# Two layers of differential attention in three step groups a head instead of four steps, on new mixing units and merge units

## The chip, the cores and the metric

The kernel runs on one core of one Trainium2 chip, as one program. The metric is the time on the device in microseconds (us), the median of several runs. An earlier stage (a transformer block with sparse attention, retention and a gated feed-forward part) comes first and takes the first third of the span; two more layers of another kind follow. The change touches only these two layers.

## The reference, cut to what matters

A layer makes a pooled branch, a convolution branch and an attention branch, gates and merges them, and goes on with an MLP. All of it is in float32. The attention is the part that the change regroups:

```python
def diff_attention(q1, q2, k1, k2, v, lam):       # S=512, 4 heads, d=64, dv=128
    nb = s_ // Q_BLOCK                            # Q_BLOCK = 128: four query blocks
    scale = d_ ** -0.5
    key_chunk = jnp.arange(s_) // CHUNK           # CHUNK = 64

    def one_block(args):
        qb1, qb2, bi = args
        q_chunk = (bi * Q_BLOCK + jnp.arange(Q_BLOCK)) // CHUNK
        mask = key_chunk[None, :] <= q_chunk[:, None]

        def probs(q, k):
            s = jnp.einsum('bhqd,bhkd->bhqk', q, k).astype(jnp.float32) * scale
            return jax.nn.softmax(jnp.where(mask, s, NEG_INF), axis=-1)

        att = probs(qb1, k1) - lam * probs(qb2, k2)
        return jnp.einsum('bhqk,bhkd->bhqd', att.astype(v.dtype), v)
    ...
# in each of the two layers, from proj = rms_norm(h) @ w_in:
    y_a = multiscale_pool(a_in, pool_w, pool_scale)          # windows 2, 4, 8, 16
    y_b = c_b * causal_depthwise_conv(c_c * c_x, conv_w)
    y_c = (rms_norm(diff_attention(...), sub_norm_g) * (1.0 - lam_init))
    merged = g_a * (y_a @ w_pool_out) + g_b * (y_b @ w_conv_out) + g_c * (y_c @ w_attn_out)
    h = h + merged @ w_o
```

Query block i sees the keys of blocks 0 to i, so its step works on 128, 256, 384 or 512 columns.

## The kernel before

**Units.** All big products are cut into units of 1024 weight columns in SBUF. A weight goes through three engines before TensorE uses it: SyncE loads it into `raw`, ScalarE copies it rounded to `w_hi` (L414), GpSimd subtracts to get `w_lo` (L357), and TensorE runs for each of 8 tiles three matmuls of 128x512: L775, L776 and L777. So a unit is 24 matmuls. ScalarE makes `w_hi` three units ahead, at the place in its own program that belongs to the current unit (`ahead`), and only when TensorE is done with the unit that had the buffer. GpSimd has nothing but `w_lo` to do in these layers, four instructions a unit.

**The mixing stage.** In each layer 16 mixing units ("slots" 0 to 15, `L_MIX`) make the inputs of the pooled and the convolution branch. They alternate between two PSUM banks, so slot j may start only when VectorE has taken slot j-2 out of its bank (L1279, in `mix_in`). VectorE runs in the order of its own loop over k: at k it takes out slot k-1 and works on it (`mix`). The slots 0, 2, 4 and 6 hold the pooled groups 3, 2, 1 and 0: a chain of 4, 3, 2 and 1 window additions (L1962), then L1968, L1972 and L1975, which writes `rg`. At tile 3 of slots 2, 4, 6 and 8 TensorE stops for a matmul that reads this `rg` (L1195). The slots 8 to 15 are four pairs "c" and "b" of the convolution.

**The merge stage.** 36 merge units follow (n = 0 to 35), 12 for each of three branches. In each six, four are gate projections and two are products with the branch outputs. Into this stage VectorE also places, in layer 0, the final norm of the earlier stage (`late_norm`): squares at n = 1, 2, 3, 7 and 8 (L2047, L2051), which TensorE sums at n = 9 by a matmul at tile 1 (L810).

**The attention steps.** Four heads of four steps are spread over both stages. A step goes around all engines:

- TensorE `attention_scores` (L1137): two score products, one for each half of the difference, into the two banks of `both`
- VectorE `step_maxima`: mask on the diagonal block (L1465), maximum (L1468), its negative scaled (L1471)
- ScalarE `softmax_step` (L528): an exponential with its sum for each half
- VectorE `step_probs`: reciprocal of the sums (L1925), second half scaled by lambda (L1927), the difference (L1930)
- TensorE `attention_transposes` (L1149), at tile 5 of a slot; ScalarE copies them to `pt` (L537); TensorE `attention_values` (L1161), after the slot. It issues the scores of the next step first.

In the mixing stage VectorE does step k/2 at every even k, around the `mix_in` of that k; the transposes and values stand at every odd slot. In the merge stage VectorE does a step at n = 0, 3, ..., 21 and TensorE closes it at n = 2, 5, ..., 23. After the last step of a head, `attention_out` copies the head's sum out (L2006) and squares it (L2009); TensorE sums the squares (L810) at tile 7 of slot 8 and at tile 6 of n = 1 and 13, and ScalarE's root of it goes on to `head_inverse` and `head_out`.

No scheduler is at work: each engine's order is the order in which its code is written, and an engine that waits holds back all that stands behind it.

## Time and profile before

| | |
|---|---|
| median of 3 runs | 2618.01 us (2617.67 to 2618.27) |
| the profiled execution | 2617.76 us |
| its span, first to last instruction | 2616.0 us |
| TensorE busy with matmuls | 2579.2 us, 99% of the span |
| VectorE busy | 1564.7 us, 60% |
| GpSimd busy | 1515.9 us, 58% |
| ScalarE busy | 840.2 us, 32% |
| mean granted TensorE clock | 0.998 |

The execution's own time is 1.76 us more than its span. "Busy" of TensorE counts overlapping matmuls once. The mixing stage of layer 0 runs from about 989 to 1098 us of the span and that of layer 1 from about 1838 to 1947 us; the merge stages follow each. In the timeline a row gives the start, the duration, the engine, the source line, what is written and read, how many instructions are merged into the row, and in brackets how long the engine sat idle before it and what ended that.

### The profile page before, as it was taken

The numbers are of one execution on the slowest core, as the hardware profiler recorded it, in microseconds if no ns is written. First come the engines' busy times: TensorE is split into PE (matmuls) and PEld (weight loads), VectorE is DVE, ScalarE is ACT, GpSimd is POOL, SyncE is SP. The second block draws the span as 40 slices with busy tenths as digits, with TensorE's granted clock in tenths as the row PEclk, the third lists the DMA queues.
The fourth block names the chain that finished last, engine by engine and source line by source line (L and its number), as shares of the span: only waits on it lengthen the run. The fifth ranks groups of instructions, "written<-read, shape, count | busy, mean of one in ns | idle before, by whom it ended". The sixth has DMA issues, their size and how long they took to land.

```text
span 2616.0 us, 32859 instructions
## 1 busy us (share of the span) xinstructions
PE 2579.2 (99%) x11707; PEld 2066.1 (79%) x11707; DVE 1564.7 (60%) x2092; ACT 840.2 (32%) x1156; POOL 1515.9 (58%) x1820
## 2 busy tenths in 40 slices
PE   7999999999999999999999999999999999999999
PEld 6767777888888877777888888877777788888887
DVE  6767774388474768855584432757883548443274
ACT  5444433233222332355321111134334432111112
POOL 6634436566666754545566655764454556665576
PEclk9999999999999999999999999999999999999999
DMA  5311113222322222122222222232222222222223
GB/s 195 122 49 59 55 65 113 97 81 96 113 96 97 97 103 81 66 96 81 105 97 97 97 96 96 96 113 88 80 69 92 97 92 94 104 97 93 96 96 125
DMA packets 36829, 247.44 MB, mean 95 GB/s; under 512 B 4464, under 2 KB 4848, under 8 KB 7792
## 3 DMA queue, kind: packets, MB, share of 16 engines
q1 hardware_dynamic: 34704, 238.57, 25.5%
q10 hardware_dynamic: 2016, 7.35, 0.8%
q8 instruction: 76, 1.25, 0.2%
q14 instruction: 33, 0.27, 0.0%
HBM read 243.81 MB, written 2.10 MB: 94 GB/s over the span
## 4 chain that ended last, share of the span: by engine, by line
PE 86%; DVE 9%; ACT 2%; POOL 1%; issue 1%; DMA 1%; DVEq 0%; ACTq 0%; SPq 0%
PE bank L775 17%; PE bank L777 17%; PE bank L776 17%; PE both L775 10%; PE both L777 9%; PE both L776 9%; PE bank L810 1%; POOL w_lo L357 1%; PE both L958 1%; DMA raw<-stream 1%; DVE small L1468 1%; PE bank L945 1%; PE both L1137 1%; PE bank L1161 1%; PE bank L977 1%
## 5 line engine op out<-in xcount | busy, mean ns | idle before, releaser
L357 POOL TENSOR_TENSOR w_lo<-raw,w_hi 128x256 fp32r<-128x256 f32 x1784 | 1493.5, 869 | 1003.6 <-ACT w_hi L414 1003.1
L414 ACT ACTIVATE w_hi<-raw 128x1024 fp32r<-128x1024 f32 x446 | 469.0, 1057 | 989.4 <-PE bank L777 495.1
L775 PE MATMUL bank<-a_hi,w_hi 128*128 128x512 f32 x1544 | 631.6, 409 | 4.2 <-POOL w_lo L357 4.2
L777 PE MATMUL bank<-a_hi,w_lo 128*128 128x512 f32 x1544 | 603.3, 391 | 0.0
L776 PE MATMUL bank<-a_lo,w_hi 128*128 128x512 f32 x1544 | 602.4, 390 | 0.0
L775 PEld LDWEIGHTS bank<-a_hi,w_hi 128*128 128x128 f32 x1544 | 290.4, 188 | 77.4 <-issue 16.3
L776 PEld LDWEIGHTS bank<-a_lo,w_hi 128*128 128x128 f32 x1544 | 290.8, 188 | 63.2 <-issue 7.9
L777 PEld LDWEIGHTS bank<-a_hi,w_lo 128*128 128x128 f32 x1544 | 290.2, 188 | 62.7
L775 PE MATMUL bank<-y_hi,w_hi 128*128 128x512 f32 x696 | 272.4, 391 | 0.0
L777 PE MATMUL bank<-y_hi,w_lo 128*128 128x512 f32 x696 | 270.9, 389 | 0.0
L776 PE MATMUL bank<-y_lo,w_hi 128*128 128x512 f32 x696 | 270.8, 389 | 0.0
L775 PE MATMUL both<-a_hi,w_hi 128*128 128x512 f32 x656 | 259.5, 396 | 0.8 <-DVE a_lo L1771 0.5
L777 PE MATMUL both<-a_hi,w_lo 128*128 128x512 f32 x656 | 255.4, 389 | 0.0
L776 PE MATMUL both<-a_lo,w_hi 128*128 128x512 f32 x656 | 255.3, 389 | 0.0
L775 PE MATMUL both<-y_hi,w_hi 128*128 128x512 f32 x504 | 197.3, 391 | 4.6 <-DVE y_lo L1594 2.7
L777 PE MATMUL both<-y_hi,w_lo 128*128 128x512 f32 x504 | 196.8, 391 | 0.0
L776 PE MATMUL both<-y_lo,w_hi 128*128 128x512 f32 x504 | 196.7, 390 | 0.0
L776 PEld LDWEIGHTS bank<-y_lo,w_hi 128*128 128x128 f32 x696 | 130.7, 188 | 27.4 <-issue 0.5
L777 PEld LDWEIGHTS bank<-y_hi,w_lo 128*128 128x128 f32 x696 | 130.6, 188 | 27.3
L775 PEld LDWEIGHTS bank<-y_hi,w_hi 128*128 128x128 f32 x696 | 130.6, 188 | 27.3 <-issue 0.5
L775 PEld LDWEIGHTS both<-a_hi,w_hi 128*128 128x128 f32 x656 | 123.1, 188 | 29.5 <-issue 2.8
L776 PEld LDWEIGHTS both<-a_lo,w_hi 128*128 128x128 f32 x656 | 123.2, 188 | 27.1 <-issue 2.2
(306 smaller groups left out, 2944.6 us busy)
## 6 DMA issues: line engine op xcount, KB each, us to landing
raw<-stream SPq DMA_DIRECT2D x223, 1024.0 KB, 4.8
h<-xT SPq DMA_DIRECT2D x8, 256.0 KB, 6.0
h<-xT ACTq DMA_DIRECT2D x1, 2048.0 KB, 7.9
outT<-h SPq DMA_DIRECT2D x8, 256.0 KB, 2.3
h<-decay ACTq DMA_DIRECT2D x1, 1024.0 KB, 4.7
h<-rope ACTq DMA_DIRECT2D x1, 1024.0 KB, 9.3
prob<-pT ACTq DMA_DIRECT2D x2, 512.0 KB, 4.2
par<-par ACTq DMA_DIRECT2D x2, 408.0 KB, 2.9
```

The lines of the kernel that those rows point to most:

```text
L357: pool.tensor_tensor(w_lo[:, s, part], raw[:, s, part], w_hi[:, s, part], ALU.subtract).then_inc(lo_done, 1)
L414: act.activation(w_hi[:, s, cols], raw[:, s, cols], ACT.Copy).then_inc(hi_done, 1)
L775: pe.matmul(dst, w_hi[:, s, cols], rhs_hi(k), start=start and k == 0, stop=False)
L776: pe.matmul(dst, w_hi[:, s, cols], rhs_lo(k), start=False, stop=False)
L777: ins = pe.matmul(dst, w_lo[:, s, cols], rhs_hi(k), start=False, stop=stop and k == nk - 1)
L810: pe.matmul((b_r1 if dst is None else dst)[:, :], ones if w is None else w, ssum[:, :] if src is None else src, start=True, stop=True)\
L945: ins = pe.matmul(dst[:, a * P:S], rv[:, a, e * P:(e + 1) * P], rp[:, at:at + n], start=a == 0, stop=a == QT - 1, skip_group_check=True)
L958: ins = pe.matmul(dst[:, 0:n], (q_turned if half != g else qt)[at, cols], k_sw[g][at, 0:n], start=True, stop=True)
L977: ins = pe.matmul(b_o[rows, col], v_sw[g][:, a, rows], pt[:, half, a * P:(a + 1) * P], start=a == 0, stop=a == i, skip_group_check=True)
L1137: ins = pe.matmul(dst[:, 0:n], qn[rows, hd, i * P:(i + 1) * P], kn[rows, hd, 0:n], start=True, stop=True)
L1161: ins = pe.matmul(b_o[:, i * P:(i + 1) * P], vn[:, hd, a, :], pt[:, 0, a * P:(a + 1) * P], start=a == 0, stop=a == i, skip_group_check=True)
L1468: V.tensor_reduce(small[:, 8:10], scores[:, :, 0:n], AX.X, ALU.max)\
```

## The change

The four steps of a head become three groups: steps 0 and 1 together, step 2, step 3. In the first group step 0 has columns 0 to 127 and step 1 columns 128 to 383 of the same banks and tiles. TensorE issues the scores, transposes and values of both steps together. VectorE masks both diagonal blocks in one instruction, takes two maxima, scales four numbers at once, takes four reciprocals at once, and has two instructions of each of the others. ScalarE runs four exponentials and one copy of 384 columns.

There are now 12 groups a layer instead of 16 steps. Six lie in the mixing stage: VectorE does them at k = 0, 3, 5, 8, 11 and 13, and TensorE closes them at slots 2, 4, 7, 10, 12 and 15. Six lie in the merge stage: VectorE at n = 0, 3, 7, 12, 15 and 19, TensorE at n = 2, 6, 11, 14, 18 and 23. Nothing else moves.

```diff
+STEP_GROUPS = [((0, 0), (1, P)), ((2, 0),), ((3, 0),)]
+MIX_STEPS, MIX_VALUES = [0, 3, 5, 8, 11, 13], [2, 4, 7, 10, 12, 15]
+MERGE_STEPS, MERGE_VALUES = [0, 3, 7, 12, 15, 19], [2, 6, 11, 14, 18, 23]
...
+                def attention_step(group):
+                    parts = []
+                    for o, (i, at) in enumerate(STEP_GROUPS[group % 3]):
+                        cols = slice(at, at + (i + 1) * P)
+                        parts += [(prob[:, e, cols], (b_s0, b_s1)[e][:, cols], 2 * o + e) for e in range(2)]
+                    softmax_step(parts, 64 ** -0.5)
...
-                    for e, dst in enumerate((b_s0, b_s1)):
-                        rows = slice(64 * e, 64 * (e + 1))
-                        ins = pe.matmul(dst[:, 0:n], qn[rows, hd, i * P:(i + 1) * P],
-                                        kn[rows, hd, 0:n], start=True, stop=True)
+                    for i, at in STEP_GROUPS[group % 3]:
+                        n = (i + 1) * P
+                        for e, dst in enumerate((b_s0, b_s1)):
+                            rows = slice(64 * e, 64 * (e + 1))
+                            ins = pe.matmul(dst[:, at:at + n], qn[rows, hd, i * P:(i + 1) * P],
+                                            kn[rows, hd, 0:n], start=True, stop=True)
...
+                def step_maxima(group):
+
+                    steps_in = STEP_GROUPS[group % 3]
+                    V.wait_ge(scores_ready, score.due())
+                    blocks = scores.rearrange("p e (b c) -> p e b c", c=P)
+                    first = steps_in[0][0]
+                    diag = blocks[:, :, first:3:2, :] if len(steps_in) > 1 else blocks[:, :, first:first + 1, :]
+                    mask = chunk.unsqueeze(1).unsqueeze(1).to_broadcast([P, 2, len(steps_in), P])
+                    V.tensor_tensor(diag, diag, mask, ALU.add).then_inc(vector_step, steps.up())
+                    V.wait_ge(vector_step, steps.now())
+                    for o, (i, at) in enumerate(steps_in):
+                        V.tensor_reduce(small[:, 8 + 2 * o:10 + 2 * o], scores[:, :, at:at + (i + 1) * P],
+                                        AX.X, ALU.max).then_inc(vector_step, steps.up())
...
-                    if k % 2 == 0:
-                        step_maxima(k // 2)
+                    if k in MIX_STEPS:
+                        step_maxima(MIX_STEPS.index(k))
                     if k > 0:
                         mix_in(k - 1)
                     if k < 2:
                         qk_out(6 + k)
-                    if k % 2 == 0:
-                        step_probs(k // 2)
+                    if k in MIX_STEPS:
+                        step_probs(MIX_STEPS.index(k))
```

VectorE at k = 0 of the mixing stage of layer 0, before: from the mask of step 0 (`both<-both,cst`) to the first window addition (`tb<-ta`) of pooled group 3.

```order
L1465 TENSOR_TENSOR both<-both,cst 128x2x128
L1468 TENSOR_REDUCE small<-both 128x2
L1471 TENSOR_SCALAR small<-small 128x2
L1891 RECIPROCAL tb<-tb 128x512
L1894 SCALAR_TENSOR_TENSOR work<-ta,par,tb 128x512
L1925 RECIPROCAL small<-small 128x2
L1927 TENSOR_SCALAR prob<-prob,small 128x128
L1930 SCALAR_TENSOR_TENSOR prob<-prob,small 128x128
L1279 TENSOR_TENSOR ta<-bank,rstd 128x512
L1891 RECIPROCAL tile_c<-tile_c 128x512
L1894 SCALAR_TENSOR_TENSOR work<-td,par,tile_c 128x512
L1962 TENSOR_TENSOR tb<-ta 128x512
```

The same stretch after the change, up to the reciprocal behind `mix_in` of slot 0 (L1292 now):

```order
L1940 TENSOR_TENSOR both<-both,cst 128x4x128
L1943 TENSOR_REDUCE small<-both 128x2 x2
L1947 TENSOR_SCALAR small<-small 128x4
L1904 RECIPROCAL tb<-tb 128x512
L1907 SCALAR_TENSOR_TENSOR work<-ta,par,tb 128x512
L1956 RECIPROCAL small<-small 128x4
L1960 TENSOR_SCALAR prob<-prob,small 128x128
L1960 TENSOR_SCALAR prob<-prob,small 128x256
L1965 SCALAR_TENSOR_TENSOR prob<-prob,small 128x128
L1965 SCALAR_TENSOR_TENSOR prob<-prob,small 128x256
L1292 TENSOR_TENSOR ta<-bank,rstd 128x512
L1904 RECIPROCAL tile_c<-tile_c 128x512
```

Three more instructions, and a mask of twice the size, now stand ahead of pooled group 3.

VectorE at k = 3, before: slot 2 (pooled group 2) is taken out and its window additions follow at once.

```order
L1279 TENSOR_TENSOR ta<-bank,rstd 128x512
L1962 TENSOR_TENSOR tb<-ta 128x512
L1962 TENSOR_TENSOR td<-tb 128x512
L1962 TENSOR_TENSOR tb<-td 128x512
L1968 SCALAR_TENSOR_TENSOR rg<-tb,ta 128x512
L1972 TENSOR_TENSOR rg<-tb,cst 128x16
L1975 TENSOR_TENSOR rg<-rg,ta 128x16
```

VectorE at k = 3 after the change:

```order
L1940 TENSOR_TENSOR both<-both,cst 128x2x128
L1943 TENSOR_REDUCE small<-both 128x2
L1947 TENSOR_SCALAR small<-small 128x2
L1292 TENSOR_TENSOR ta<-bank,rstd 128x512
L1956 RECIPROCAL small<-small 128x2
L1960 TENSOR_SCALAR prob<-prob,small 128x384
L1965 SCALAR_TENSOR_TENSOR prob<-prob,small 128x384
L1999 TENSOR_TENSOR tb<-ta 128x512
L1999 TENSOR_TENSOR td<-tb 128x512
L1999 TENSOR_TENSOR tb<-td 128x512
L2005 SCALAR_TENSOR_TENSOR rg<-tb,ta 128x512
L2009 TENSOR_TENSOR rg<-tb,cst 128x16
```

The step of 384 columns has moved from k = 4 to k = 3, in front of the chain that ends in `rg`, and its mask waits for scores that TensorE issues only when slot 2 is over.

## Rows read from the trace of the kernel before

**Rows 1.** The page, busy time of TensorE: us, share of span, instructions.

```profile
PE 2579.2 (99%) x11707; PEld 2066.1 (79%) x11707; DVE 1564.7 (60%) x2092; ACT 840.2 (32%) x1156; POOL 1515.9 (58%) x1820
```

**Rows 2.** TensorE's waits, whole execution: engine, line, releaser: us, times, longest.

```profile
PE bank L810 <- DVE ssum L2009: 1.8, 2, 0.9
```

**Rows 3.** Timeline of TensorE, mixing stage of layer 0 and the end of n = 23.

```profile
988.71 0.39 PE L777 MATMUL bank<-a_hi,w_lo 128*128 128x512 f32 x1
...
989.79 0.39 PE L776 MATMUL bank<-a_lo,w_hi 128*128 128x512 f32 x1
...
1001.60 0.70 PE L1137 MATMUL both<-work 64*128 64x256 f32 x4
...
1007.18 0.40 PE L776 MATMUL bank<-a_lo,w_hi 128*128 128x512 f32 x1
...
1013.54 0.39 PE L777 MATMUL bank<-a_hi,w_lo 128*128 128x512 f32 x1
...
1245.80 0.40 PE L777 MATMUL bank<-y_hi,w_lo 128*128 128x512 f32 x1
...
1247.16 0.39 PE L776 MATMUL bank<-a_lo,w_hi 128*128 128x512 f32 x1
```

**Rows 4.** Timeline of TensorE, slot 2 of layer 0, tile 2 and the stop.

```profile
1004.40 0.39 PE L777 MATMUL bank<-a_hi,w_lo 128*128 128x512 f32 x1
1005.99 1.12 PE L1195 MATMUL bank<-rg,par 128*128 128x512 f32 x2 [1.20 <-DVE rg L1975]
```

**Rows 5.** VectorE by line and shape, mixing stage of layer 0: busy us, mean ns.

```profile
L1468 DVE TENSOR_REDUCE small<-both 128x2 f32<-128x512 f32 x2 | 1.4, 691 | 0.1
...
L1930 DVE SCALAR_TENSOR_TENSOR prob<-prob,small 128x256 f32<-128x256 f32 x2 | 1.0, 484 | 0.1
...
L1927 DVE TENSOR_SCALAR prob<-prob,small 128x256 f32<-128x256 f32 x2 | 0.8, 414 | 0.1
```

**Rows 6.** Timeline of VectorE, pooled group 3 and the mask after it.

```profile
1001.92 0.69 DVE L1962 TENSOR_TENSOR tb<-ta 128x512 f32<-128x512 f32 x1
...
1005.97 0.43 DVE L1465 TENSOR_TENSOR both<-both,cst 128x256 f32<-128x256 f32 x1
```

**Rows 7.** Timeline of GpSimd, slots 2 and 3 of layer 0.

```profile
1009.41 7.47 POOL L357 TENSOR_TENSOR w_lo<-raw,w_hi 128x256 fp32r<-128x256 f32 x8 [9.26 <-ACT w_hi L414]
```

**Rows 8.** Timeline of VectorE, pooled group 2, then step 2.

```profile
1011.95 0.91 DVE L1962 TENSOR_TENSOR tb<-ta 128x512 f32<-128x512 f32 x1
...
1014.04 1.11 DVE L1962 TENSOR_TENSOR tb<-td 128x512 f32<-128x512 f32 x1
...
1017.20 0.43 DVE L1465 TENSOR_TENSOR both<-both,cst 128x256 f32<-128x256 f32 x1
...
1021.57 0.75 DVE L1941 TENSOR_SCALAR y_hi<-bank,par 128x512 fp32r<-128x512 f32 x1
```

**Rows 9.** Timeline of VectorE, first step of head 1 at slot 8.

```profile
1044.65 0.43 DVE L1465 TENSOR_TENSOR both<-both,cst 128x256 f32<-128x256 f32 x1 [2.46 <-PE both L1137]
...
1048.45 1.13 DVE L2009 TENSOR_TENSOR ssum<-tile_c 128x512 f32<-128x512 f32 x1
```

**Rows 10.** Timeline of TensorE, the sum of squares in slot 8.

```profile
1051.17 1.02 PE L810 MATMUL bank<-ssum,cst 128*128 128x512 f32 x2
```

**Rows 11.** Timeline of VectorE, from step 2 of head 1 to slot 14.

```profile
1073.47 0.41 DVE L1465 TENSOR_TENSOR both<-both,cst 128x256 f32<-128x256 f32 x1
...
1096.30 0.69 DVE L1279 TENSOR_TENSOR tb<-bank,rstd 128x512 f32<-128x512 f32 x1
```

**Rows 12.** Timeline of VectorE, squares at n = 12 of layer 0.

```profile
1182.21 1.18 DVE L2009 TENSOR_TENSOR ssum<-tile_c 128x512 f32<-128x512 f32 x1
```

**Rows 13.** Timeline of TensorE, their sum at n = 13.

```profile
1183.50 1.07 PE L810 MATMUL bank<-ssum,cst 128*128 128x512 f32 x2
```

**Rows 14.** Timeline of VectorE, n = 8 of layer 0 and the next mask.

```profile
1153.10 0.69 DVE L1279 TENSOR_TENSOR work<-bank,rstd 128x512 f32<-128x512 f32 x1 [1.76 <-PE bank L777]
...
1155.28 0.43 DVE L1465 TENSOR_TENSOR both<-both,cst 128x256 f32<-128x256 f32 x1
```

More of the change, by code:

```diff
@@ L110, with group_width @@
 SWAP_RET = [(i + 16) % 32 for i in range(32)]
+def group_width(group):
+    i, at = STEP_GROUPS[group % 3][-1]
+    return at + (i + 1) * P
 class Count:
@@ L1139, in attention_scores, with attention_transposes @@
                     ins.then_inc(scores_ready, score.up())
-                def attention_transposes(s):
-                    if s > 0 and s % QT == 0:
-                        pe.wait_ge(head_root_ready, layer * LAYER_HEADS + s // QT)
-                    if (layer, s) == (0, 11):
+                def attention_transposes(group):
+                    if group > 0 and group % 3 == 0:
+                        pe.wait_ge(head_root_ready, layer * LAYER_HEADS + group // 3)
+                    if (layer, group) == (0, 8):
@@ L1157, in attention_values @@
                     pe.wait_ge(probs_copied, ptr.due())
-                    if i == 0:
+                    if group % 3 == 0:
                         pe.wait_ge(attention_out_read, ofree.due())
-                    for a in range(i + 1):
-                        ins = pe.matmul(b_o[:, i * P:(i + 1) * P], vn[:, hd, a, :],
-                                        pt[:, 0, a * P:(a + 1) * P], start=a == 0, stop=a == i,
-                                        skip_group_check=True)
+                    for i, at in STEP_GROUPS[group % 3]:
+                        for a in range(i + 1):
+                            ins = pe.matmul(b_o[:, i * P:(i + 1) * P], vn[:, hd, a, :],
+                                            pt[:, 0, at + a * P:at + (a + 1) * P], start=a == 0, stop=a == i,
+                                            skip_group_check=True)
@@ L1924, in step_probs @@
+                def step_probs(group):
+                    steps_in = STEP_GROUPS[group % 3]
+                    n = 2 * len(steps_in)
                     V.wait_ge(exp_ready, ex.due())
-                    V.reciprocal(small[:, 12:14], small[:, 4:6]).then_inc(vector_step, steps.up())
+                    V.reciprocal(small[:, 12:12 + n], small[:, 4:4 + n]).then_inc(vector_step, steps.up())
                     V.wait_ge(vector_step, steps.now())
-                    V.tensor_scalar(prob[:, 1, 0:n], prob[:, 1, 0:n], small[:, 13:14], small[:, 18:19],
-                                    ALU.mult, ALU.mult).then_inc(vector_step, steps.up())
@@ L1929, in step_probs @@
-                    V.wait_ge(vector_step, steps.now())
-                    V.scalar_tensor_tensor(out=prob[:, 0, 0:n], in0=prob[:, 0, 0:n],
-                                                  scalar=small[:, 12:13], in1=prob[:, 1, 0:n],
-                                                  op0=ALU.mult, op1=ALU.add)\
-                                                      .then_inc(probs_ready, prb.up())
+                    for o, (i, at) in enumerate(steps_in):
+                        cols = slice(at, at + (i + 1) * P)
+                        V.tensor_scalar(prob[:, 1, cols], prob[:, 1, cols], small[:, 13 + 2 * o:14 + 2 * o],
+                                        small[:, 18:19], ALU.mult, ALU.mult).then_inc(vector_step, steps.up())
@@ new lines, in step_probs @@
+                    for o, (i, at) in enumerate(steps_in):
+                        cols = slice(at, at + (i + 1) * P)
+                        V.wait_ge(vector_step, steps.now() - (len(steps_in) - 1 - o))
+                        ins = V.scalar_tensor_tensor(out=prob[:, 0, cols], in0=prob[:, 0, cols],
+                                                     scalar=small[:, 12 + 2 * o:13 + 2 * o],
+                                                     in1=prob[:, 1, cols], op0=ALU.mult, op1=ALU.add)
+                        if o < len(steps_in) - 1:
+                            ins.then_inc(vector_step, steps.up())
@@ L1934, in step_probs @@
+                    ins.then_inc(probs_ready, prb.up())
                     V.wait_ge(probs_ready, prb.now())
```

74 lines of the change are left out of this document (35 added, 39 removed).

## The prediction

> **What bounds the kernel now.** I read the page first: TensorE is busy 99% of the span [rows 1]. So nothing that merely eases VectorE, ScalarE or GpSimd shortens the program; only TensorE's own work counts, and the moments at which it stands. Next I read who makes it stand. In these stages there are two places a layer, alike in both layers. In slot 2 it waits 1.20 us for the `rg` of pooled group 3 [rows 4], and at n = 1 it waits 0.9 us for the squares of head 1 [rows 2]. Both times VectorE is late. Last I read the timelines of TensorE and VectorE beside each other, to see how much earlier than needed VectorE finishes elsewhere. That slack is what this change spends.
>
> TensorE's pace: from 1007.18 to 1013.54 it starts 28 matmuls of 512 columns, 0.227 us each [rows 3]. A unit of 24 takes 5.44 us, its first three tiles 2.04.
>
> **The change part by part.** All times are against the profiled execution, 2617.76 us (span 2616.0 and 1.76 around it).
>
> *TensorE's work.* Columns and matmuls stay the same. Scores of 128 columns alone stretch the distance from an L777 to the second matmul after it from 0.45 to 1.08 us (988.71 to 989.79), so they cost 0.62. Four blocks of values alone stretch it to 1.36 (1245.80 to 1247.16): 0.90, or 0.22 a block [rows 3]. Scores of 128 columns stream for 0.21 us, two passes of 128 at twice 0.227/512 us a column; 0.41 is for getting in and out. If steps 0 and 1 are issued together, the second entry is saved wholly or not at all: 0 to 0.41. Between two products the weights still have to be loaded, so I take the middle, 0.21, eight times: **-1.7 us** (0 to -3.3). Values have no such fixed part (0.22 a block also when they are four), so nothing is saved there.
>
> The Trainium skill, page "TensorEngine Tiling (Array Packing)", section "Instruction Overhead", says that every matmul has an overhead of about 60 cycles. By it, with as many matmuls as before, nothing at all would be saved, and the sum below would be 1.7 us higher. The 0.41 us in the trace lies at the change between products and not in each of them.
>
> *Slot 2: group 0 in front of pooled group 3.* At k = 0 VectorE now also does step 1. It has no idle time between there and L1975. Added: a mask of 512 instead of 256 columns (0.69 instead of 0.43, taking the 0.69 of the 512-column reduction): 0.27; a reduction of 512 columns, 0.69 [rows 5] and 0.03 between instructions; L1927 and L1930 on 256 columns, 0.41 and 0.48 [rows 5] and 0.07. That is 1.95 us. The two more exponentials are hidden behind L1891 and L1894. So `rg` comes 1.95 us later. TensorE however arrives 0.55 us sooner: transposes, values of step 0 and scores of 256 columns (0.12 + 0.22 + 0.83) no longer lie before it, and of the first group only the second scores do (0.83 less the 0.21 saved, 0.62). What it has not yet done there it does later, so these 0.55 are idle time on top. A third part: before, GpSimd was idle while these window additions ran. Its 9.26 us of idle time ended at 1009.41, because ScalarE's `w_hi` stood behind the exponentials of k = 2 [rows 7]. An addition took 0.69 then, and pooled group 3 took 4.05 (1001.92 to 1005.97) [rows 6]. While GpSimd works (from 1009.41 on), the same addition takes 1.11 [rows 8]. At k = 2 no exponential stands before `w_hi` any more, so GpSimd starts about when slot 1 ends, beside pooled group 3. Three to four of five instructions are then 0.42 longer: 1.4 (0 to 2.1). Sum for slot 2: **+3.9** (2.5 to 4.6).
>
> *Slot 4: step 2 in front of pooled group 2.* Before, the window additions of k = 3 followed at once on `mix_in`; now the step of 384 columns is ahead of them, and its scores are issued after slot 2 only. From the end of slot 2: scores of 384 columns are there after 1.1 us (those of 256 columns take 0.70 after an entry of about 0.1, 1001.60 [rows 3], 0.21 more for the columns, and a wake-up). Mask, maximum, `mix_in`, exponentials and L1927, L1930 took 4.37 (1017.20 to 1021.57), pooled group 2 took 5.25 (1011.95 to 1017.20) [rows 8], or 3.3 when GpSimd is quiet (4.05 less one addition of 0.73). Together 10.7 (8.8). TensorE reaches tile 3 of slot 4 after scores 1.05, three blocks of values 0.67, slot 3 with 5.44 and 2.04: 9.2. GpSimd has a unit of `w_lo` to make just then, as in rows 8, so I take the long value: **+1.6** (0 to 1.9).
>
> *Slot 6: step 3 in front of pooled group 1.* The same with one addition less (-1.1) and a step that is longer by 128 columns in every instruction (+0.7), while TensorE gets 0.2 more for scores: **+1.3** (0 to 1.8).
>
> *Slot 8: group 3 in front of `attention_out`.* From the mask at 1044.65 to the end of the squares at 1048.45 + 1.13 it took 4.93 us [rows 9]; TensorE asked for them at 1051.17, 1.5 us later [rows 10]. Now mask and reduction are 0.99 longer, the exponentials 0.8 (four instead of two, no longer mostly under `mix_in`), L1927 and L1930 0.97: 2.76 less 1.5 is **+1.3** (0.9 to 2.0).
>
> *Slot 15.* It needs slot 13 taken out of its bank. Before, the chain from the step of 384 columns (1073.47) to the take-out of slot 14 (1096.30) had no idle time but the exponentials: 22.8 us [rows 11]. The same chain now runs from k = 11 to k = 14 and holds one take-out and a half of `head_inverse` more: 25.4, and 26.5 us to its end counted from slot 10's. TensorE needs 25.8 for slots 11 to 14 with their small products. With some more contention: **+1.0** (-0.2 to 2.0).
>
> *n = 1 and n = 13: group 6 and group 9 in front of `attention_out`.* At n = 13 the squares were ready at 1183.39 and asked for at 1183.50 [rows 12, 13]. L1927 and L1930 of step 1 are 0.97 longer (the exponentials lie before the take-out of the gate unit): **+0.9** (0.4 to 1.4). At n = 1 VectorE used to be late from slot 14 and 15 and TensorE stood 0.9 us [rows 2]. It has caught up now, since its last step is at k = 13, and is late only by the same 0.9: **-0.2** (-0.7 to 0.3).
>
> *Layer 0 only, n = 9.* The sum of squares of the late norm stands at tile 1 of n = 9. Before, values and scores of 512 columns (1.9 us) lay between n = 8 and n = 9. Now they lie after n = 11. VectorE needs the take-out and the last square and addition, 1153.10 to 1155.28 [rows 14], plus 0.3 from the end of the unit: 2.5. TensorE is there after 0.68: **+1.9** (1.8 to 2.7). At n = 6 the gating of n = 4 is late for the same reason, no values after n = 5: **+0.5** (0 to 0.9).
>
> *The sum.* In a layer 3.9 + 1.6 + 1.3 + 1.3 + 1.0 + 0.9 - 0.2 = 9.8; twice 19.6. Layer 0 adds 2.4, the products save 1.7: **+20.3 us**. TensorE has nothing idle behind these stages in which this could vanish. The ends: low 2 x 2.9 + 1.8 - 3.3 = +4.3, high 2 x 14 + 3.6 = +31.6. 2617.76 + 20.3 = 2638.1; the median of before is 0.25 above the profiled execution, so 2638.3 is expected of a median. I say 2638.
>
> **The rivals.**
>
> *A, the cover holds (about no change, 2623 us).* The pooled chains run beside an idle GpSimd: slots 4 and 6 cost nothing, slot 15 is in time, and slot 2 and the squares cost their lower bounds. That is the low end, +4.3. For it: VectorE stood idle 2.46 us before the mask at slot 8 [rows 9], so it isn't short of time in the mean. Against it: the order is fixed, and the idle time lies before the masks, because the scores come late; it can't be used for what stands behind them. A measurement can tell about 0.2% (5.2 us) from no change, so this end counts as the same. Chance 0.13.
>
> *B, VectorE is relieved (faster, about 2612 us).* Each head saves VectorE a mask, a small product and a reciprocal, each with its start-up. The late `rg` in slot 2 and the late squares at n = 1 vanish, 2.1 us a layer [rows 2, 4], and with the products 5.9 us are won: 2611.9. It decides at k = 0: VectorE would need 2 us of idle time between the first step and L1962. The chain there is without a gap, so only the part at n = 1 is likely. Chance 0.04.
>
> The Trainium skill, page "VectorE: DVE Perf Modes", section "The TRN2 errata — SBUF-src ops pay a fixed extra latency per instruction", says that a large tile pays this once and many small tiles pay it each time. That speaks for rival B: fewer instructions. By the rows the second half of the group still pays for its own reductions and scalings.
>
> *C, contention and lateness add up (2650 us).* VectorE is late at k = 13 already, so slots 14 and 15 and n = 6 wait more: the high end, +31.6. Chance of more than 2646: 0.10.
>
> *D, the forecast:* +5.2 to +28, chance 0.73.
>
> **How the numbers follow.** The range 2625 to 2646 leaves out B, nearly all of A and the end of C, together about 0.2. Slower by over 0.2% is D and C, 0.83; the same is A, 0.13; faster is B, 0.04.
>
> **What would show it.** In the profile after: TensorE waits for `rg` in slots 2 (about 5 us), 4 and 6 (1 to 2 each) in both layers, and for the squares in slot 8, at n = 1 and 13 (about 1 each) and, in layer 0, at n = 9 (about 1.9). GpSimd's idle time before its work at slot 2 is shorter, and the window additions of group 3 take 1.1 us. The distance around the first scores grows from 1.08 to about 1.7. Wrong would be: no wait at slots 4 and 6 with additions of 0.7 us (rival A), or a wait in slot 2 below 1 us (B).

## The result, and the profile after

| | before | after |
|---|---|---|
| median | 2617.84 us (2617.54 to 2618.27, 4 runs) | 2646.62 us (2645.27 to 2648.56, 4 runs) |
| ratio | | 1.0111 (95%: 1.0096 to 1.0125) |
| profiled execution | 2617.76 us | 2648.56 us |
| its span | 2616.0 us | 2646.8 us |
| mean granted TensorE clock | 0.998 | 0.995 |

The change makes the kernel 28.8 us slower by the medians, and 30.8 us between the two profiled executions. I had predicted +20.3 and a range up to 2646, so the direction was right and the time lies just above the range. The profiled execution of after is the slowest of its four, 1.9 us above their median. After ran in the first job only; between the jobs of this document the kernel before moves by 0.3 us. One execution of `e_slot2` took 9207.83 us and is in none of the medians below.

The page of after, busy time of each engine, answers to [rows 1]:

```profile
PE 2585.9 (98%) x11707; PEld 2070.5 (78%) x11707; DVE 1564.2 (59%) x2068; ACT 830.1 (31%) x1141; POOL 1521.9 (58%) x1820
```

TensorE has exactly as many matmuls as before and yet is busy 6.7 us longer. The other 24 us of the 30.8 are time in which it stands. VectorE is as busy as before: its 24 instructions less don't show.

TensorE's waits of after, whole execution (engine, line, releaser: us, times, longest). Of these, before had 2.4 us in two waits for `rg` and 1.8 in two for the squares [rows 2, 4]:

```profile
PE bank L1208 <- DVE rg L2012: 18.6, 6, 5.7
...
PE bank L821 <- DVE ssum L2046: 5.7, 6, 1.2
...
PE bank L821 <- DVE td L2088: 2.7, 1, 2.7
```

Six waits for `rg` are slots 2, 4 and 6 of both layers. Six for the squares are slot 8, n = 1 and n = 13. One, for `td`, is the late norm at n = 9. These are the places that the prediction named.

Timeline of TensorE of after, slot 2 of layer 0: the last matmul of tile 2, the stop, and what follows. It answers to [rows 4]:

```profile
1004.25 0.39 PE L788 MATMUL bank<-a_hi,w_lo 128*128 128x512 f32 x1
1010.37 2.07 PE L1208 MATMUL bank<-rg,par 128*128 128x512 f32 x2 [5.73 <-DVE rg L2012]
1011.46 1.42 PE L786 MATMUL bank<-a_hi,w_hi 128*128 128x512 f32 x1
1012.67 0.63 PE L787 MATMUL bank<-a_lo,w_hi 128*128 128x512 f32 x1
1013.10 0.63 PE L788 MATMUL bank<-a_hi,w_lo 128*128 128x512 f32 x1
1013.52 0.63 PE L786 MATMUL bank<-a_hi,w_hi 128*128 128x512 f32 x1
...
1014.26 0.40 PE L788 MATMUL bank<-a_hi,w_lo 128*128 128x512 f32 x1
```

Two things stand here. The wait is 5.73 us instead of 1.20. And behind it the matmuls start 0.43 us apart instead of 0.227. From the product to the last row it is 3.89 us. The same stretch before took 2.10: 0.56 and 0.63 around the product, and four distances of 0.227. So 1.8 us are lost after the wait is over.

That is the clock, as the windows of the trace show. A row gives the stretch, its length, the busy time and count of PE (matmuls), PEld (weight loads), DVE (VectorE), ACT (ScalarE) and POOL (GpSimd), then the granted TensorE clock, the DMA share and GB/s. Of after, the stretch behind the stop in slot 2 and n = 9 of layer 0, and slots 2 and 4 of layer 1:

```profile
1011.50:1013.90 2.40, 2.40 (x6) 1.55 (x5) 1.31 (x2) 0.00 (x0) 0.00 (x0) 0.50 0.27 109
1171.00:1174.60 3.60, 3.60 (x10) 2.46 (x9) 0.00 (x0) 2.88 (x4) 2.38 (x4) 0.53 0.55 232
1877.30:1880.50 3.20, 3.20 (x8) 2.11 (x7) 1.50 (x2) 0.00 (x0) 0.00 (x0) 0.50 0.23 95
1895.60:1898.50 2.90, 2.90 (x8) 1.94 (x7) 1.50 (x2) 0.00 (x0) 0.33 (x1) 0.56 0.47 107
```

A granted clock of 0.50 is the lower of TensorE's two levels, 1.2 instead of 2.4 GHz. In these two layers it falls four times in this execution, each time at a stop, and never in the kernel before. By the distances of the matmuls the falls cost 1.8 us (slot 2) and 1.6 (n = 9) in layer 0, 2.4 (slot 2) and 1.6 (slot 4) in layer 1, together 7.4 us. The mean clock agrees: 0.995 instead of 0.998 is 0.003 x 2646.8 = 8 us (from rounded figures).

VectorE of after, k = 0 and 1 of layer 0, up to the `rg` of pooled group 3, with GpSimd beside it. They answer to [rows 6, 7]:

```profile
1003.78 1.28 DVE L1907 SCALAR_TENSOR_TENSOR work<-td,par,tile_c 128x512 f32<-128x512 f32 x1
1005.09 1.10 DVE L1999 TENSOR_TENSOR tb<-ta 128x512 f32<-128x512 f32 x1
...
1007.35 1.09 DVE L1999 TENSOR_TENSOR tb<-td 128x512 f32<-128x512 f32 x1
1008.48 0.69 DVE L1999 TENSOR_TENSOR td<-tb 128x512 f32<-128x512 f32 x1
...
1010.14 0.17 DVE L2012 TENSOR_TENSOR rg<-rg,ta 128x16 f32<-128x16 f32 x1
```

```profile
1003.77 4.13 POOL L366 TENSOR_TENSOR w_lo<-raw,w_hi 128x256 fp32r<-128x256 f32 x4 [2.15 <-ACT w_hi L423]
```

GpSimd works from 1003.77 to 1007.90. In that time the additions take 1.10 us; the one that begins after it takes 0.69. The prediction had expected this: no exponential stands before `w_hi` at k = 2 any more, so GpSimd starts earlier.

**The ledger.** I compared the distances of TensorE's matmuls, place by place, between the two traces (us, filling and draining of the pipeline included; the two layers where they differ):

| place | predicted | measured | of it the clock |
|---|---|---|---|
| slot 2, a layer | 3.9 | 6.3, 6.9 | 1.8, 2.4 |
| slot 4, a layer | 1.6 | 2.3, 3.9 | 0, 1.6 |
| slot 6, a layer | 1.3 | 1.8 | 0 |
| slot 8, a layer | 1.3 | 1.3 | 0 |
| slot 15, a layer | 1.0 | 0.4 | 0 |
| n = 1, a layer | -0.2 | +0.3 | 0 |
| n = 13, a layer | 0.9 | 0.85 | 0 |
| n = 9, layer 0 | 1.9 | 4.6 | 1.6 |
| n = 6, layer 0 | 0.5 | 0.4 | 0 |
| TensorE's products | -1.7 | -3.1 | |

The column sums to 30.7. The two profiled executions are 30.8 us apart, and 0.6 of that already lies ahead of these two layers. Nothing large is missing; what follows asks whether each line has the cause that I gave it.

### The profile page after: what moved, and what is told of

It is laid out like the page before. It is cut to its first block, busy times and chain, and to the rows that moved or that the text cites. A ratio compares the mean times of both kernels' runs of the same rounds, so it can differ in the third digit from the quotient of the medians.

```text
span 2646.8 us, 32797 instructions
## 1 busy us (share of the span) xinstructions
PE 2585.9 (98%) x11707; PEld 2070.5 (78%) x11707; DVE 1564.2 (59%) x2068; ACT 830.1 (31%) x1141; POOL 1521.9 (58%) x1820
## 4 chain that ended last, share of the span: by engine, by line
PE 85%; DVE 10%; ACT 2%; issue 1%; POOL 1%; DMA 1%; DVEq 0%; SPq 0%; ACTq 0%
PE bank L786 17%; PE bank L788 16%; PE bank L787 16%; PE both L786 9%; PE both L787 9%; PE both L788 9%; PE bank L821 1%; POOL w_lo L366 1%; PE both L969 1%; PE both L1149 1%; ACT prob L537 1%; PE bank L956 1%; DVE prob L1965 1%; PE bank L988 1%; DMA raw<-stream 1%
## 5 line engine op out<-in xcount | busy, mean ns | idle before, releaser
L788 PE MATMUL bank<-a_hi,w_lo 128*128 128x512 f32 x1544 | 604.6, 392 | 0.0
L788 PEld LDWEIGHTS bank<-a_hi,w_lo 128*128 128x128 f32 x1544 | 291.1, 189 | 62.8
L788 PE MATMUL bank<-y_hi,w_lo 128*128 128x512 f32 x696 | 270.9, 389 | 0.0
L788 PE MATMUL both<-a_hi,w_lo 128*128 128x512 f32 x656 | 255.5, 389 | 0.0
L788 PE MATMUL both<-y_hi,w_lo 128*128 128x512 f32 x504 | 196.7, 390 | 0.0
L788 PEld LDWEIGHTS bank<-y_hi,w_lo 128*128 128x128 f32 x696 | 130.6, 188 | 27.2
```

The source lines that it names most:

```text
L788: ins = pe.matmul(dst, w_lo[:, s, cols], rhs_hi(k), start=False, stop=stop and k == nk - 1)
```

## The experiments

The theory: TensorE loses the time at the named stops, because VectorE's groups now stand ahead of what it waits for; and a part, some 7 us, is lost behind the stops to its lower clock. The rival to the second half: the slow stretches are something that comes with the stops anyhow (a refill, late weights), and would stay if the engine were kept busy. The rival to the first: single places are worth less than their waits, since the time is given back further on.

All ratios are to the kernel before in the same job (medians 2617.63 to 2617.89 us). What a run wins is counted from the median of after, 2646.62 us.

### The clock: TensorE kept busy while it waits

`e_fill` leaves every wait where it is, but lets TensorE run matmuls into an idle bank before each of the long ones. Nobody reads their results, so the kernel does more work than after.

```diff
+FILLERS = {2: 24, 4: 9, 6: 7}
...
+                def filler(j, times):
+                    s, cols = conv_unit_slot(j % 4)
+                    for _ in range(times):
+                        pe.matmul(b_cmp[:, :], w_hi[:, s, cols.start:cols.start + P], a_hi[:, 0, :],
+                                  start=True, stop=True)
...
+                    if k == 3 and slot in FILLERS:
+                        filler(slot, FILLERS[slot])
...
+                        filler(n % 12, 11)
```

> The changed kernel with nothing moved; while TensorE would stand in slots 2, 4 and 6 and at n = 9 of layer 0, it runs 24, 9, 7 and 11 more matmuls of 512 columns whose result nobody reads (extra work, nothing left out). Theory 1 (about 8 us of the loss are TensorE's granted clock, which falls to 0.5 after the waits in slot 2, in slot 4 of layer 1 and at n = 9): the fillers end before the data come (24 x 0.227 = 5.4 of 5.7 us idle), the clock stays at 1.0, so in spite of the added work the time falls by 4 to 8 us, to 2639 to 2643. Rival (the loss is idle time alone): no gain, 2646 to 2649, since the same data are waited for.

Measured: 2641.16 us (2639.92 to 2641.43), ratio 1.0089 (1.0072 to 1.0105), mean clock 0.998. TensorE's timeline at slot 2 of layer 0:

```profile
1008.92 1.12 PE L1217 MATMUL bank<-rg,par 128*128 128x512 f32 x2 [0.34 <-DVE rg L2022]
1009.48 0.79 PE L787 MATMUL bank<-a_hi,w_hi 128*128 128x512 f32 x1
1010.11 0.39 PE L788 MATMUL bank<-a_lo,w_hi 128*128 128x512 f32 x1
1010.34 0.40 PE L789 MATMUL bank<-a_hi,w_lo 128*128 128x512 f32 x1
```

`rg` is as late as ever, but behind it the distances are 0.56, 0.63 and 0.23 as before, and in neither layer does the clock fall any more. With 40 more matmuls in each of two mixing stages and 11 at n = 9 the kernel is 5.5 us faster than after. The clock is shown as a cause of its own. Its size is read better from the traces than from the medians. From the last unit matmul ahead of slot 0 of layer 0 to the last one of the program, after takes 30.2 us more than the kernel before, and `e_fill` 23.0: about 7.1 us are won there, against 7.4 in the ledger. The medians show less because the profiled execution of after is a slow one of its four; whether the others had fewer falls isn't known.

### The mixing stage: where the groups stand

`e_slots46` moves two groups one k later and takes the waits in slots 4 and 6 away. It changes nothing in slot 2.

```diff
-MIX_STEPS, MIX_VALUES = [0, 3, 5, 8, 11, 13], [2, 4, 7, 10, 12, 15]
+MIX_STEPS, MIX_VALUES = [0, 4, 6, 8, 11, 13], [2, 5, 7, 10, 12, 15]
```

> The changed kernel with the single steps put behind the pooled groups again: VectorE's steps at k = 0, 4, 6, 8, 11, 13, TensorE's values at slots 2, 5, 7, 10, 12, 15. Theory (waits in slots 4 and 6 come only from the place of the step before the window additions): both waits go, 2.3 + 1.8 us in layer 0 and 4.4 + 1.8 in layer 1 with its clock, time 2636 (2634 to 2639). Rival (VectorE has too much to do there in any order): under 3 us gained, and the waits appear in slots 5 to 8.

Measured: 2637.41 us (2636.91 to 2638.49), ratio 1.0073 (1.0056 to 1.009). TensorE's waits of this kernel:

```profile
PE bank L1208 <- DVE rg L2012: 11.5, 2, 5.7
```

Four of the six waits are gone, 7.1 us, and with them the fall of the clock in slot 4 of layer 1. 9.2 us are won of an expected 10.6, and the ledger has 9.8 for these places. Nothing large is given back further on.

`e_slot2` moves these and the first group of the mixing stage too, from k = 0 to k = 2. No step is then ahead of pooled group 3.

```diff
-MIX_STEPS, MIX_VALUES = [0, 3, 5, 8, 11, 13], [2, 4, 7, 10, 12, 15]
+MIX_STEPS, MIX_VALUES = [2, 4, 6, 8, 11, 13], [3, 5, 7, 10, 12, 15]
...
-                        attention_step(0)
```

> As the one before, but group 0 is also behind pooled group 3: steps at k = 2, 4, 6, 8, 11, 13, values at slots 3, 5, 7, 10, 12, 15. Theory: the wait in slot 2 goes wholly (7.8 us a layer with clock, before the change 1.5), so 26 us in all, 2620 (2617 to 2623). Rival (the longer group is late wherever it is): a wait of 1 to 3 us reappears in slot 3 or 4, 2625 or more.

Measured: 2625.52 us (2624.87 to 2626.63, 7 runs), ratio 1.0029 (1.0018 to 1.004): 21.1 us won, but 5.5 fewer than I had expected. TensorE's timeline at slot 2 of layer 0, the last matmul of tile 2 and the stop, tells why:

```profile
1003.06 0.39 PE L787 MATMUL bank<-a_hi,w_lo 128*128 128x512 f32 x1
1005.04 1.13 PE L1207 MATMUL bank<-rg,par 128*128 128x512 f32 x2 [1.60 <-DVE rg L2011]
```

VectorE's timeline of the same kernel, from the take-out of slot 0 to `rg`:

```profile
996.08 0.69 DVE L1291 TENSOR_TENSOR ta<-bank,rstd 128x512 f32<-128x512 f32 x1 [1.80 <-PE bank L787]
996.80 3.35 DVE L1903 RECIPROCAL tile_c<-tile_c 128x512 f32<-128x512 f32 x1
...
1004.82 0.17 DVE L2011 TENSOR_TENSOR rg<-rg,ta 128x16 f32<-128x16 f32 x1
```

With nothing of the attention ahead of it, VectorE waits 1.80 us for slot 0 and then still needs 8.9 us (996.08 to 1004.99): the take-out, the last part of the keys (a reciprocal of 3.35 us and a product), and pooled group 3. TensorE needs only slot 1 and three tiles, 7.5 us. VectorE's timeline before, the end of the same chain:

```profile
1005.76 0.17 DVE L1975 TENSOR_TENSOR rg<-rg,ta 128x16 f32<-128x16 f32 x1
```

Slot 0 starts 0.1 us earlier in this kernel than before. Counted from there, `rg` comes 0.8 us earlier than before, because no step is ahead of it; but TensorE is at the stop 1.2 us earlier (1003.06 against 1004.40 [rows 4]), because it no longer has a step's transposes, values and scores to do in slot 1. So the wait is 1.60 us instead of 1.20. Taking the attention away on both engines doesn't remove it: the product simply stands too early, and that bounds what any place for the groups can win there. The clock fell only at n = 9 in this kernel, where the wait of 2.7 us was left.

### The merge stage: the late norm at n = 9, and a trade

`e_merge` puts the merge groups on places where the kernel before had steps, with values after n = 8 again. The mixing stage is that of after. With the values, TensorE's wait for the root of the late norm moves from the transposes of n = 11 to n = 13, here and in `e_group_only`, `e_best` and `e_best2`.

```diff
-MERGE_STEPS, MERGE_VALUES = [0, 3, 7, 12, 15, 19], [2, 6, 11, 14, 18, 23]
+MERGE_STEPS, MERGE_VALUES = [0, 3, 6, 12, 15, 18], [2, 5, 8, 14, 17, 20]
```

> The changed kernel with the old places in the merge stage: steps at n = 0, 3, 6, 12, 15, 18, values at n = 2, 5, 8, 14, 17, 20 (and TensorE's wait for the late root moved to n = 13). Theory: in layer 0 the wait at n = 9 (3.5 us idle and drained, 1.4 us slow clock) and the one at n = 6 (0.4) go, nothing changes in layer 1: 2641.4 (2640 to 2643). Rival (the late norm is late by itself): under 1.5 us gained.

Measured: 2645.23 us (2643.97 to 2645.87), ratio 1.0102 (1.0085 to 1.0119): 1.4 us won where I expected 5, and the executions of the two kernels overlap. The waits at n = 9 and n = 6 are indeed gone. But at n = 13 a new one has come in both layers, 1.85 us and 1.76 instead of 0.63. TensorE's and VectorE's timelines of this kernel in layer 0:

```profile
1197.45 1.10 PE L821 MATMUL bank<-ssum,cst 128*128 128x512 f32 x2 [1.85 <-DVE ssum L2046]
```

```profile
1191.66 0.69 DVE L1292 TENSOR_TENSOR work<-bank,rstd 128x512 f32<-128x512 f32 x1 [2.16 <-PE bank L788]
...
1192.60 1.27 DVE L1960 TENSOR_SCALAR prob<-prob,small 128x128 f32<-128x128 f32 x2
1193.79 1.71 DVE L1965 SCALAR_TENSOR_TENSOR prob<-prob,small 128x128 f32<-128x128 f32 x2
...
1196.33 0.98 DVE L2046 TENSOR_TENSOR ssum<-tile_c 128x512 f32<-128x512 f32 x1
```

VectorE isn't late at n = 12 as a whole: it waits 2.16 us for the gate unit of n = 12. But what follows that unit, the second half of the first group, the copy and the squares, runs beside a busy GpSimd. L1960 and L1965 take 1.27 and 1.71 us; in after, where GpSimd's turn comes at another time, they take 0.94 and 0.86. So the later values of after, which cost 4.6 us at n = 9, save about 1.2 at n = 13 in each layer. I had taken these two places for independent. That it is GpSimd which makes the difference at n = 13 is read from these durations; no run changed it alone. The places together give 4.6 + 0.4 - 2.4 = 2.6 us. The profiled executions are 2.7 apart, the medians 1.4, within the spread of the runs of after.

### The squares

`e_out_first` only lets VectorE copy out and square the last head before it finishes the new group's probabilities.

```diff
-                    if k in MIX_STEPS:
-                        step_probs(MIX_STEPS.index(k))
...
+                    if k in MIX_STEPS:
+                        step_probs(MIX_STEPS.index(k))
...
-                        if stepped:
-                            step_probs(6 + MERGE_STEPS.index(n))
...
+                        if stepped:
+                            step_probs(6 + MERGE_STEPS.index(n))
```

> The changed kernel with VectorE's order turned at k = 8 and n = 0, 12: attention_out first, then step_probs. Theory (the waits for the squares in slot 8, at n = 1 and 13 are only the longer L1960 and L1965 of the group in front): all three go, 1.05 + 1.2 + 0.62 us idle a layer and 0.1 each for the refilled pipeline, 2640.3 (2639 to 2642). Rival (the values come late too): under 2 us gained.

Measured: 2641.18 us (2640.89 to 2642.63), ratio 1.0091 (1.0076 to 1.0107). All six waits for `ssum` of L2046 are gone from the waits, 5.7 us, and 5.4 are won. Confirmed: `step_probs` ahead of `attention_out` was their cause. The run moves all of `step_probs`, so it doesn't tell the second half of the group from the first, which already stood there in the kernel before and left it a wait of 0.9 us at n = 1 [rows 2].

### Grouping without moving

`e_group_only` has groups, but at places of the old steps: of a head's four places it drops one.

```diff
+MIX_STEPS, MIX_VALUES = [0, 2, 4, 8, 10, 12], [1, 3, 5, 9, 11, 13]
+MERGE_STEPS, MERGE_VALUES = [0, 3, 6, 12, 15, 18], [2, 5, 8, 14, 17, 20]
```

> Only the grouping: steps 0 and 1 of a head together, on the old places (steps at k = 0, 2, 4, 8, 10, 12 and n = 0, 3, 6, 12, 15, 18; values at slots 1, 3, 5, 9, 11, 13 and n = 2, 5, 8, 14, 17, 20). Theory: TensorE's own work falls by 3.1 us; in slot 2 it waits 1.5 us more a layer than in the kernel before, at n = 13 0.9 more, at slots 14 to n = 1 0.5 less: 2618.5, and up to 2622.5 if the clock falls in slot 2. Rival (the grouping is what costs, not the places): 2630 or more.

Measured: 2624.8 us (2624.46 to 2625.77, 9 runs), ratio 1.0026 (1.0016 to 1.0036). It is above my 2618.5 to 2622.5 and below the rival's 2630. So 7.0 of the 28.8 us come with the grouping at places of the old steps, and 21.8 with the new places. The waits of this kernel:

```profile
PE bank L821 <- DVE ssum L2046: 8.3, 6, 2.1
...
PE bank L1206 <- DVE rg L2012: 3.8, 2, 1.9
```

And windows behind the stops in slot 2, at n = 1 and at n = 13 of layer 0:

```profile
1009.00:1011.50 2.50, 2.50 (x8) 1.91 (x7) 1.75 (x5) 2.18 (x5) 0.20 (x1) 0.50 0.02 7
1112.00:1116.00 4.00, 3.86 (x15) 2.87 (x16) 1.27 (x3) 3.11 (x5) 2.76 (x4) 1.00 0.75 262
1189.60:1192.60 3.00, 3.00 (x9) 2.29 (x8) 0.92 (x2) 1.95 (x3) 0.00 (x0) 0.51 0.20 85
```

The first group of a head is what hurts: 1.9 us in slot 2, 1.8 to 1.9 at n = 13, 2.1 at n = 1 of layer 0. And two falls of the clock, about 3 us together, are again on top. My 2618.5 had too little for the waits and nothing for the clock, which I had only as a chance of 2622.5.

### GpSimd beside the window additions

`e_hold` tests the third part of slot 2's term, the slower window additions. ScalarE's `w_hi` at k = 2 waits until pooled group 3 is done, so that GpSimd starts later.

```diff
+                    if k == 2:
+                        act.wait_ge(pooled_three, layer + 1)
...
+                        if j == 3:
+                            V.sem_inc(pooled_three, 1)
```

> The changed kernel, but ScalarE makes the rounded weights of k = 2 only when pooled group 3 is written, so that GpSimd has nothing to do beside its window additions. Theory (three of them at 1.10 instead of 0.69 us and L1907 at 1.28 instead of 0.75 are GpSimd's doing): the wait in slot 2 is 1.8 us shorter in each layer, 2643 (2641.5 to 2644.5). Rival (VectorE is slow there for another reason): durations unchanged, 2646 to 2648.

VectorE's and GpSimd's timelines of this kernel, slot 2 of layer 0:

```profile
1003.08 0.75 DVE L1910 SCALAR_TENSOR_TENSOR work<-td,par,tile_c 128x512 f32<-128x512 f32 x1
1003.87 0.69 DVE L2002 TENSOR_TENSOR tb<-ta 128x512 f32<-128x512 f32 x1
...
1007.71 0.17 DVE L2015 TENSOR_TENSOR rg<-rg,ta 128x16 f32<-128x16 f32 x1
```

```profile
1009.11 2.79 POOL L367 TENSOR_TENSOR w_lo<-raw,w_hi 128x256 fp32r<-128x256 f32 x4 [8.19 <-ACT w_hi L424]
```

The mechanism is shown: every addition is 0.69 again, and the idle time in slot 2 is 3.99 and 3.98 us, 1.74 less, as expected. Both engines gain: an instruction of GpSimd takes 0.70 us (2.79 / 4) alone and 1.03 (4.13 / 4) beside VectorE. The Trainium skill, page "SBUF — State Buffer", section "SBUF: two separate sides", has the port pair that the two share as an exclusive lock, on which the loser waits for the whole instruction. By that rule, as an estimate from the two times alone, an addition and a subtraction would take 0.69 + 0.70 = 1.39 us between them. In the trace of after the additions start 1.13 us apart, so the trace doesn't bear out a lock for the whole instruction.

Yet the time is 2647.41 us (2645.57 to 2647.94), ratio 1.0111 (1.0095 to 1.0126): nothing won, where I expected 3.6. Its mean clock is 0.994. The trace shows where it went. The clock falls in five places, after's four and slot 4 of layer 0, which costs 1.6 us more there. And the slow stretch behind the product of slot 2 is longer than in after, since the product comes 1.74 us earlier and the clock comes back only a little earlier. The window behind the product in layer 0:

```profile
1008.00:1013.00 5.00, 5.00 (x12) 3.28 (x12) 2.19 (x3) 1.03 (x1) 2.79 (x4) 0.50 0.00 0
```

By the distances of the matmuls slot 2 gains 1.1 and 1.3 us in the two layers and not 1.74. From slot 0 of layer 0 to the end `e_hold` is then 1.0 us ahead of after; the medians, 0.8 the other way, can't tell this from nothing.

`e_hold_fill` has the edit of `e_hold` and the filler matmuls of `e_fill`, fewer of them in slot 2, whose wait is shorter. It is to be read against `e_fill`:

```diff
-FILLERS = {2: 24, 4: 9, 6: 7}
+FILLERS = {2: 17, 4: 9, 6: 7}
```

> The delayed rounded weights of e_hold and the filling matmuls of e_fill together (17, 9, 7 and 11 of them; their result is not read). e_hold took 1.74 us of idle time out of slot 2 of each layer without getting faster. Theory (a varying number of clock falls hid the gain): with the clock kept at 1.0 the 3.5 us show, 2637.7 against 2641.2 of e_fill (2636.5 to 2639). Rival (the weights held back cost as much elsewhere): 2640.5 to 2642.5.

Measured: 2636.86 us (2636.74 to 2637.47), ratio 1.0074 (1.006 to 1.0087), clock 0.999. That is 4.3 us under `e_fill`, for 3.5 of waits. With the clock out of the way, the contention is worth in time about what it is worth in the waits.

### A version that is faster than both

`e_best` puts all the repairs together: no group at k = 0, the groups at every second k, the old merge places, `attention_out` first.

```diff
+MIX_STEPS, MIX_VALUES = [2, 4, 6, 8, 10, 12], [3, 5, 7, 9, 11, 13]
+MERGE_STEPS, MERGE_VALUES = [0, 3, 6, 12, 15, 18], [2, 5, 8, 14, 17, 20]
```

> All mends together: groups, steps at k = 2, 4, 6, 8, 10, 12 with values at slots 3, 5, 7, 9, 11, 13, the old places in the merge stage, attention_out ahead of step_probs. Theory: none of the waits of the kernel before is left in these stages (2.8 us a layer), and TensorE's work falls by 3.1 us: 2609 (2607 to 2611). Rival (a wait takes the place of each removed): 2615 or more.

Measured: 2612.37 us (2611.86 to 2612.96, 11 runs), ratio 0.9979 (0.997 to 0.9988). That is 3.4 us above the 2609 that I expected, and outside my range: I had expected no wait to be left, and 1.60 us in slot 2 are, in both layers. `e_best2` also moves the product of slot 2 from tile 3 to tile 7:

```diff
-                    if k == 3 and slot in (2, 4, 6, 8):
+                    if k == (7 if slot == 2 else 3) and slot in (2, 4, 6, 8):
```

> e_best with the product of pooled group 3 at tile 7 of slot 2 instead of tile 3. In e_best TensorE still stands 1.6 us there, because the take-out of slot 0, the last normalised key and the window additions take 9.0 us from the end of slot 0 and TensorE is there after 7.5. Theory: 2.7 us later it never waits, 1.7 us a layer are won: 2609 (2608 to 2610.5). Rival (VectorE, which waits for the product, becomes late in slots 3 and 4): 2611 or more.

Measured: 2610.3 us (2609.62 to 2610.77, 7 runs), ratio 0.9972 (0.996 to 0.9983), 7.3 us under the kernel before, and 2.1 under `e_best` where I expected 3.4. A little comes back one product later: its waits for `rg` are in slot 4.

```profile
PE bank L1205 <- DVE rg L2011: 0.6, 2, 0.3
```

How much of it is the grouping? `e_before_mended` gives the kernel before, with its four steps a head, the same two repairs, the later product in slot 2 and `attention_out` first.

> The kernel before with its 16 ungrouped steps on their old places and two of the mends: the product of pooled group 3 at tile 7 of slot 2, and attention_out ahead of step_probs. Theory: its waits in slot 2 (1.5 us with the refilled pipeline) and at n = 1 (1.2) go in both layers, 2612.6 (2611.5 to 2614); the difference of 3 to 3.5 us to e_best2 is what the grouping itself is worth on TensorE. Rival (the grouping is worth nothing and the places did all): 2609, as e_best2.

Measured: 2612.67 us (2612.06 to 2613.1, 11 runs), ratio 0.9981 (0.9972 to 0.999); TensorE has no wait left for `rg` or for the squares of a head. So 5.0 us of the 7.3 have nothing to do with groups. The grouping, together with the places that `e_best2` gives the groups, is worth 2.4 us, a little less than the 3.1 that TensorE's products save in after, and only if no place pays for it.

## Why the prediction was right and wrong

**Right: the direction and the places.** All waits that I named came, with the same releasers, and none came that I hadn't named. VectorE with 40% of idle time was no protection, since its idle time lies before the masks, where scores come late, and the products wait for what stands behind the masks. Rival A (cover) and rival B (VectorE relieved) are out: the additions in slot 4 took 1.1 us, and VectorE's busy time didn't change at all (1564.7, 1564.2). The wait in slot 2, "about 5 us", was 5.73; `e_hold` shows its part from contention, 1.74 us against the 1.4 that the prediction took for it. Slots 8, n = 13 and n = 6 came out within 0.1 us, slot 15 with 0.4 inside its bounds. VectorE at slot 4 of after, the first addition and the last instruction before the product:

```profile
1022.40 1.11 DVE L1999 TENSOR_TENSOR tb<-ta 128x512 f32<-128x512 f32 x1
...
1027.60 0.65 DVE L2012 TENSOR_TENSOR rg<-rg,ta 128x16 f32<-128x16 f32 x1
```

**Wrong: that an idle microsecond costs one.** The step that failed is the one that isn't in the sum. Every term counted the time in which TensorE stands, and the sum took its pace afterwards as 0.227 us. It was 0.43 for a while behind four of the stops. That is 7.4 of the 10.5 us that were missing between +20.3 and +30.8; the granted clock shows it, and `e_fill` got 5.5 us back by the medians, 7.1 by the traces, with more work. The one wait of this kind before, 1.20 us in slot 2, had no such tail. The window of before behind it:

```profile
1006.50:1010.00 3.50, 3.50 (x16) 2.72 (x15) 2.89 (x7) 1.97 (x5) 0.59 (x1) 1.00 0.03 5
```

I never asked whether a wait of 5 us would leave the clock at 1.00 as well. Rival C had the right size for the wrong reason: it looked for more lateness in slots 14, 15 and n = 6.

**Wrong by size: some terms.** The idle part of slot 2 was 4.5 instead of 3.9 a layer, slot 4 2.3 instead of 1.6, slot 6 1.8 instead of 1.3, n = 1 +0.3 instead of -0.2. In all four there is a busy GpSimd beside the late instructions. At slot 2 that is half of it: I had counted contention on the additions, but not on L1907 just ahead of them, 1.28 instead of 0.75. The other half is that TensorE came to the stop 0.8 us sooner and not 0.55, mostly because the scores save 0.39 and not 0.21. In slots 4 and 6 the two small instructions that end the chain take up to 0.65 us instead of 0.17. Slots 4 and 6 were also summed wrongly: their steps give 10.7 - 9.2 = 1.5 and 1.6 - 1.1 + 0.7 - 0.2 = 1.0, not 1.6 and 1.3, so more was missing there than the terms show. At n = 9 the wait was 2.72 and with the drain 3.0 us, instead of 1.9. VectorE's timeline of after, layer 0, at n = 1 and then from n = 7 to n = 8:

```profile
1117.97 1.71 DVE L1965 SCALAR_TENSOR_TENSOR prob<-prob,small 128x128 f32<-128x128 f32 x2
...
1164.74 1.11 DVE L2088 TENSOR_TENSOR td<-td,work 128x512 f32<-128x512 f32 x1
...
1168.22 0.69 DVE L1292 TENSOR_TENSOR work<-bank,rstd 128x512 f32<-128x512 f32 x1
```

At n = 1 the two instructions of L1965 take 1.71 us; at n = 13, in quieter company, 0.86. At n = 7 the squares take 1.11 each, and so the take-out at n = 8 doesn't follow the end of the unit by 0.3 us, as I had assumed, but comes when VectorE is through. Together these terms were 4.6 us short, slot 15 subtracted.

**Wrong the other way: TensorE's saving.** I took the middle between nothing and the full 0.41 us a pair of scores, 1.7 us for eight. Timeline of TensorE of after around the first pair, which answers to the first two lines of [rows 3]:

```profile
989.34 0.39 PE L788 MATMUL bank<-a_hi,w_lo 128*128 128x512 f32 x1
989.66 0.93 PE L1149 MATMUL both<-work 64*128 64x128 f32 x8
...
990.85 0.39 PE L787 MATMUL bank<-a_lo,w_hi 128*128 128x512 f32 x1
```

From the L788 to the second matmul after it are 1.51 us, 0.45 of it its own pace, so 1.06 for both scores, against 0.62 + 0.83 = 1.45 apart. That is 0.39 saved, the whole entry, eight times 3.1. The getting in and out of these products is paid once for the run and not for each. (The prediction's own formula, two passes of 128 columns at twice 0.227/512 us, makes 0.23 us and not the 0.21 that it wrote, and leaves this same 0.39.) The sum was offset by 1.4 us to the good here; it would have been further off without.

**What an experiment corrected in my account.** In the expectation of `e_slot2` I had let the wait in slot 2 go wholly with the step ahead of it; 1.60 us stay with no step there. And I had treated n = 9 and n = 13 as separate; `e_merge` shows that the place of the values moves 1.2 us a layer between them.

## What to carry to other kernels

An instruction moved in front of something that the busiest engine waits for costs its length less what that place had in hand, however idle its own engine is on average; ask for each such place when its input comes, what stands between, and which other engine slows it down just then. A stop of TensorE of some microseconds must be priced with the slower matmuls behind it, and if the stop can't be avoided, look whether work can be put into it. Before regrouping work, move the one consumer that asks too early: here moving a product by four tiles and swapping two calls gave 5 us, and the grouping with its places 2.4.

## What the runs showed of the hardware

**The clock falls at short stops too, but not at each.** In after it was at 0.50 to 0.56 behind waits of 5.73 us (both layers), 2.72 us and once 2.02 us. Slot 4 has the same wait of 2.02 us in both layers. TensorE's timeline of after, the product in layer 0 and then in layer 1:

```profile
1028.30 1.12 PE L1208 MATMUL bank<-rg,par 128*128 128x512 f32 x2 [2.02 <-DVE rg L2012]
```

```profile
1894.65 2.02 PE L1208 MATMUL bank<-rg,par 128*128 128x512 f32 x2 [2.02 <-DVE rg L2012]
```

In layer 0 the product takes 1.12 us, in layer 1 2.02 at the lower clock. `e_group_only` had a fall behind 1.90 us in slot 2 of layer 0 and none behind 1.89 us in slot 2 of layer 1, a fall behind 1.86 us at n = 13 of layer 0 and none behind 2.07 us at n = 1; `e_slot2` and `e_best` had 1.60 us in slot 2 and no fall. So the length of the stop alone doesn't decide. What does wasn't tried.

**Both engines pay for contention.** VectorE's additions go from 0.69 to 1.10 us and GpSimd's subtractions from 0.70 to 1.03 when they run side by side (`e_hold` against after), and a small shift in time (an exponential more or less before `w_hi`) decides whether they do. This made up 1.74 us of one wait.

**The 64-row score products have a fixed cost of about 0.4 us that a run of them pays once.** One pair of 128 columns costs 0.62 us, the two pairs of after 1.06 together. The four blocks of values, on 128 rows, show no such cost, 0.22 us a block [rows 3]. That it comes from the 64 rows wasn't tested.
